# Differential attention of a two-block network on one Trainium2 core: the scores of heads 1 to 3 as three rounded products, and the outputs' sums of squares as halvings on GpSimd

## The reference

```python
q = rms_norm(q, g_q) * (HEAD_DK ** -0.5)
k = rms_norm(k, g_k)
...
        s = jnp.einsum('bqhjd,bkhjd->bhjqk', qi, k).astype(jnp.float32) + bias[None, :, None]
        p = jax.nn.softmax(s, axis=-1)
        w = (p[:, :, 0] - lam * p[:, :, 1]).astype(v.dtype)
        return jnp.einsum('bhqk,bkhd->bqhd', w, v)
...
    o = rms_norm(o, g_o) * (1.0 - lam_init)
```

## Time and profile before

| | us |
|---|---|
| median of 3 runs | 2111.61 (2109.74 to 2114.71) |
| the profiled execution, its own time | 2111.26 |
| the profiled execution, its span | 2109.5 |
| attention block, first score matmul to the next block's first matmul | 314.8 to 474.8 |
| busy in the whole span | PE 2035.7 (96%), DVE 1658.3 (79%), ACT 1081.6 (51%), POOL 262.5 (12%) |

### The profile page before, as it was taken

One profiled execution on the slowest core, in us unless ns is written; L12 is line 12 of the kernel. 1 busy time (PEld: TensorE's weight loads), 2 busy tenths in 40 slices (PEclk: granted clock), 3 DMA queues, 4 the chain that ended last, 5 costly groups with the idle time before them and its releaser, 6 DMA issues. The chain is left out here.

```text
span 2109.5 us, 25237 instructions
## 1 busy us (share of the span) xinstructions
PE 2035.7 (96%) x9940; PEld 1586.0 (75%) x9940; DVE 1658.3 (79%) x1706; ACT 1081.6 (51%) x1267; POOL 262.5 (12%) x192
## 2 busy tenths in 40 slices
PE   6999999999988999999999989999999999899998
PEld 4766766777736888888888757888888876688876
DVE  5575448885686999999999769999999977855776
ACT  4388417883236777777777542112222159622134
POOL 0200000001000111111110140000000006623040
PEclk9999999999999999999999999999999999999999
DMA  7311332104489999999999741111122236433121
GB/s 292 118 40 40 125 112 85 41 1 100 163 350 348 366 401 393 401 393 399 392 394 398 212 183 43 60 60 62 58 80 100 90 114 236 160 130 120 41 80 60
DMA packets 131496, 381.95 MB, mean 181 GB/s; under 512 B 9736, under 2 KB 22568, under 8 KB 131401
## 3 DMA queue, kind: packets, MB, share of 16 engines
q1 hardware_dynamic: 117640, 341.02, 42.7%
q0 software_dynamic: 7536, 22.70, 4.4%
q10 hardware_dynamic: 6224, 16.93, 2.0%
HBM read 337.49 MB, written 43.07 MB: 180 GB/s over the span
## 5 line engine op out<-in xcount | busy, mean ns | idle before, releaser
L2992 DVE SCALAR_TENSOR_TENSOR arena<-arena,vecs 128x1023 f32<-128x1023 f32 (+14 forms) x240 | 304.5, 1269 | 7.1
L2292 DVE TENSOR_TENSOR w_low<-W,w_high 128x2048 fp32r<-128x2048 f32 x96 | 217.0, 2288 | 33.5 <-ACT w_high L2189 33.5
L2292 DVE TENSOR_TENSOR w_low<-arena,w_high 128x2048 fp32r<-128x2048 f32 x96 | 218.4, 2290 | 19.0 <-ACT w_high L2189 19.0
L2005 PE MATMUL Q<-hT_high,w_high 128*128 128x512 f32 (+1 forms) x736 | 229.4, 391 | 2.6 <-DVE hT_low L2275 1.9
L2005 PE MATMUL Q<-hT_low,w_high 128*128 128x512 f32 (+1 forms) x720 | 224.5, 390 | 0.0
L2189 ACT ACTIVATE w_high<-arena 128x2048 fp32r<-128x2048 f32 x96 | 184.2, 1920 | 73.1 <-PE Q L2080 73.1
L2005 PE MATMUL Q<-hT_high,ring_low 128*128 128x512 f32 x704 | 219.7, 390 | 0.0
L2189 ACT ACTIVATE w_high<-W 128x2048 fp32r<-128x2048 f32 x96 | 184.0, 1919 | 66.4 <-PE Q L2080 64.3
L2018 ACT ACTIVATE w_high<-W 128x1024 fp32r<-128x1024 f32 x44 | 46.5, 1058 | 251.7 <-PE Q L2005 243.0
L2005 PEld LDWEIGHTS Q<-hT_high,w_high 128*128 128x128 f32 (+1 forms) x736 | 135.0, 184 | 35.1 <-DVE hT_low L2275 2.1
L2080 PE MATMUL Q<-w_high,x_high 128*128 128x512 f32 x512 | 160.9, 396 | 0.6 <-DVE x_low L2300 0.6
(11 more groups left out here) (502 smaller groups left out, 4148.7 us busy)
## 6 DMA issues: line engine op xcount, KB each, us to landing
arena<-in_w_dram SPq DMA_DIRECT2D x48, 2048.0 KB, 11.5
W<-in_w_dram SPq DMA_DIRECT2D x48, 2048.0 KB, 12.4
W<-in_w_mod_dram SPq DMA_DIRECT2D x12, 2048.0 KB, 8.2
W<-in_w_in_dram SPq DMA_DIRECT2D x12, 2048.0 KB, 8.4
W<-in_w_out_dram SPq DMA_DIRECT2D x6, 2048.0 KB, 9.8
spill<-arena ACTq DMA_DIRECT2D x24, 512.0 KB, 2.7
W<-in_w_in_dram SPq DMA_DIRECT2D x8, 1024.0 KB, 8.8
arena<-spill SPq DMA_DIRECT2D x3, 2048.0 KB, 12.4
```

Source lines behind the costliest of these rows:

```text
L2005: ins = nc.tensor.matmul(Q[rows, 2 * pair_of(n) + half, :], w[:, k], x[:, k, HALF * half:HALF * half + HALF], start=k == 0 and w is high a ...
L2292: nc.vector.tensor_tensor(wl[:], chunk_src(r, j), wh[:].bitcast(F32), ALU.subtract).then_inc(low_v, 1)
L2992: ins = nc.vector.scalar_tensor_tensor(conf[:, i, j:], u[:, 0:S - j], w, conf[:, i, j:], ALU.mult, ALU.add)
```

## The change

For heads 1 to 3, POOL splits q and k of a head into a rounded first part (`qk_first`, two pairs of tiles in turn) and the rest (`qk_low`, written over q and k themselves), by a copy and a subtraction each. The scores of these heads are then three products each, for two halves of the keys and two maps: 12 matmuls a turn in place of 4, j being the innermost loop. Heads 1 and 2 are split at the start of the block. Head 3 is split after POOL has done the square sums of turns 0 to 13 and PE the scores of turn 15, whose tiles it takes over. ACT no longer squares: `o_ready` is raised by the scaled copy, and POOL takes the sum of squares of each output by a product and seven additions of halves, each waiting for the one before.

```diff
-        o_square = tiles(23)[:, HALF:HALF + P]
+        SPLIT_HEADS = range(1, HEADS)
+        qk_low = rounded("qk_low", 24, [P, 2 * HEADS, S])
+        qk_first = [[rounded(f"qk_first{t}", t, [P, S]) for t in pair] for pair in ((6, 21), (22, 23))]
+        qk_split = sem("qk_split")
+        o_sq = keep[:, 2 * P:3 * P]
...
+                def square_sum(i):
+                    h, t = divmod(i, NT)
+                    pool.wait_ge(o_ready, i + 1)
+                    g_link(nc.gpsimd.tensor_tensor(o_sq, o_rows[:, h, t], o_rows[:, h, t], ALU.mult))
+                    for w in (P // 2, P // 4, P // 8, P // 16, P // 32, P // 64):
+                        g_link(nc.gpsimd.tensor_tensor(o_sq[:, 0:w], o_sq[:, 0:w], o_sq[:, w:2 * w], ALU.add))
+                    g_link(nc.gpsimd.tensor_tensor(o_ssq[:, i:i + 1], o_sq[:, 0:1], o_sq[:, 1:2], ALU.add))
+
+                for n, h in enumerate(SPLIT_HEADS):
+                    if n >= 2:
+                        for i in range(2 * NT - 2):
+                            square_sum(i)
+                        pool.wait_ge(score_mm, 2 * NT * (h - 1))
+                    for side in range(2):
+                        whole, first = qk[:, HEADS * side + h], qk_first[n % 2][side]
+                        nc.gpsimd.tensor_copy(first[:], whole).then_inc(qk_split, 1)
+                        pool.wait_ge(qk_split, 4 * n + 2 * side + 1)
+                        nc.gpsimd.tensor_tensor(qk_low[:, HEADS * side + h], whole, first[:].bitcast(F32), ALU.subtract)\
+                            .then_inc(qk_split, 1)
+                for i in range(2 * NT - 2, TURNS):
+                    square_sum(i)
...
+                def split_scores(i):
...
+                    pe.wait_ge(qk_split, 4 * n + 4)
+                    for half in range(2):
+                        cols_k = slice(HALF * half, HALF * half + HALF)
+                        for p, (q, k) in enumerate(((q_first, k_first), (q_first, k_low), (q_low, k_first))):
+                            for j in range(2):
+                                if half == 0 and p == 0:
+                                    pe.wait_ge(max_ready, 2 * (i - 1) + j + 1)
+                                rows = slice(DK * j, DK * j + DK)
+                                ins = nc.tensor.matmul(Q[:, 2 * j + half, :], q[rows, P * t:P * t + P], k[rows, cols_k],
+                                                       start=p == 0, stop=p == 2)
+                                if half == 1 and p == 2:
+                                    ins.then_inc(score_mm, 1)
...
-                    nc.scalar.activation(o_rows[:, h, t], Q[:, 6 + i % 2, 0:P], ACT.Copy, scale=over_sum)
-                    if i:
-                        act.wait_ge(o_ready, i)
-                    nc.scalar.activation(o_square, Q[:, 6 + i % 2, 0:P], ACT.Square, scale=over_sum,
-                                         accum_out=o_ssq[:, i:i + 1]).then_inc(o_ready, 1)
+                    nc.scalar.activation(o_rows[:, h, t], Q[:, 6 + i % 2, 0:P], ACT.Copy, scale=over_sum)\
+                        .then_inc(o_ready, 1)
```

More of the change, by code:

```diff
@@ L1222, in _ @@
+                for i in range(2 * NT - 2, TURNS):
+                    square_sum(i)
             @block.tensor
             def _(pe):
+                def split_scores(i):
+                    h, t = divmod(i, NT)
+                    n = SPLIT_HEADS.index(h)
+                    q_first, k_first = qk_first[n % 2]
+                    q_low, k_low = qk_low[:, h], qk_low[:, HEADS + h]
+                    pe.wait_ge(qk_split, 4 * n + 4)
[10 more added lines that the diff above has]
+                                    ins.then_inc(score_mm, 1)
@@ L1224, in scores @@
                 def scores(i):
                     h, t = divmod(i, NT)
+                    if h in SPLIT_HEADS:
+                        split_scores(i)
+                        return
                     for j in range(2):
```

## The result

The changed kernel took 2117.62 us in the median of ten runs (2116.24 to 2121.87, and one of 2449.76), the kernel before 2111.35 beside it: a ratio of 1.0033, 95% interval [1.0024, 1.0043]. It is slower, by some 7 us. The run of 2449.76 had a mean granted clock of 0.791, the others 0.985 to 0.989, and the ratio leaves it out. The profiled execution took 2117.37, its span is 2115.6, 6.1 longer than before.

The account below looks back on a forecast made before the run. PE was taken to bound the attention block, with DVE next at 0.4 us of slack. Terms -5.8 + 5.0 + 2.5 + 2.6 + 2.7 + 1.7 = +8.7 on 2111.26 gave 2120 us, range 2113 to 2128.

Parts of the forecast that it names:

- C: First turns: POOL's splits of heads 1 and 2 delay DVE's weights, +5.0 us (0 to 7).
- B: Eight turns with `out_rest`: L1193 waits for POOL's product, a turn taking 5.05 against 4.73, +2.6 us.
- the clock: Behind the block's end: PE at half clock after standing still, partly hidden by a later wait, +1.7 us.
- A: Scores of heads 1 to 3: fp32r pairs shorten a turn by 0.36 to 4.37 us; 16 turns give -5.8.
- D: Turns 16 or 17: POOL's split of head 3 delays DVE, +2.5 us (0 to 5).
- the sums: Block's end: POOL's last two square sums delay the next block's start, +2.7 us (1.3 to 3.8).
- The rival without them: Scores: fp32r pairs run one after the other, +1.0 us in 24 turns, +33 in all, 2145; chance 0.06.
- half as much POOL work: Head 3's split: half the POOL work of heads 1 and 2 was taken to cost half, +2.5 us.
- DVE needs 4.61: Turns with `out_rest`: DVE's chain, L1193 included, was read as needing 4.61 us against PE's 4.73.
- POOL's work in DVE's free stretches: Attention block: POOL's instructions miss DVE's two-input work, so C and D cost 0; -4.1 us, 2107.2; chance 0.20.
- Half contention: Block: one subtraction of heads 1 and 2 and one of head 3 hit at half length; +0.9, 2112.2; chance 0.12.

Follow-up runs that it names:

- e5: Kernel before plus four copies and four subtractions of k tiles on POOL at the block's start, into scratch; ratio 1.004 [1.0027, 1.0054].
- e4: Changed kernel with squares back on ACT and each split instruction gated behind chosen turns' weights; 2104.33 us against 2110.32 for the kernel before.
- e9: Kernel before plus the eight POOL instructions of e5, gated as in e4; ratio 1.0003 [0.9994, 1.0012].
- e1: Changed kernel with squares back on ACT, so POOL only splits, ungated; 2107.86 us against 2110.32 for the kernel before.
- e2: Kernel before with only the square sums moved to POOL, scores left float32 and unsplit; ratio 1.002 [1.0011, 1.003].
- e8: Changed kernel, square sums on POOL, with only its split instructions gated as in e4; 2107.84 us against 2111.46 for the kernel before.
- e10: Kernel before plus the eight POOL instructions of e5 done twice, ungated; ratio 1.0039 [1.0025, 1.0053] against the kernel before.
- e7: e4 with map j as the outermost loop of the split scores; ratio 1.0031 [1.0017, 1.0045] against the kernel before.

## Why the prediction was right, and where its sizes were off

The mechanism, POOL and DVE holding each other for one instruction at a time, was right, and so was the sign of each term; the sum came out at 2120.0 against 2117.62 (+8.7 forecast, +6.3 between the medians). That it came so near is in part luck: C, B and the clock were 5.1 us too high together, A, D and the sums 2.9 too low, and more than a third of D is a cost that the forecast did not have, PE's half clock behind a held turn inside the block. The terms:

**A, the scores: -5.4 for -5.8.** A turn of 4.39, saving 0.34. The passes of a pair are 0.233 us apart (392.56 to 393.49, four steps), not 0.227 as in the earlier trace rows. The Trainium skill's figure ("TensorE: Matmul & The Clock Gate", section "Back-to-back issue gap"), 216 ns, is the farther one; no run here shows it. The pairs ran side by side: the rival without them, 2145, is out.

**C, splits of heads 1 and 2: +3.8 for +5.0.** L1339 was held by 2.2 us in the first turn (3.46 for 1.28), by 0.7 in the second, with 0.46 and 0.73 at L1336; the third and fourth turns were free, since there the last subtraction waited for DVE. The forecast had DVE 3.2 and then 2.2 late; it was 2.6 and 1.5. e5 shows POOL as the cause, e4 and e9 show the place.

**D, split of head 3: +4.3 for +2.5.** The step that failed is "half as much POOL work" for "half of C". The cost goes by what POOL has in flight when a turn's weights come up, and by what PE's clock does then. Turn 16 lost 2.6: a copy held L1336 by 0.65 and a subtraction L1339 by 2.2, with 0.2 of slack. The turn behind it lost 1.65, and there it was PE at half clock and not DVE, a term that the forecast put at nothing inside the block. In e1 the same work falls two turns earlier, L1324 is held by 0.86 and L1327 by 0.73, the clock stays up, and 1.4 is lost; in e4 nothing is.

**B, turns with `out_rest`: +0.3 for +2.6.** The largest miss. "DVE needs 4.61" was read from a turn in which L1193 waited a little; alone DVE needs 4.54 (e4), and without POOL the eight turns would have gained 1.8 (e1, e4). And POOL's product does not cost its length: after L1339 it ends 0.26 later (432.99 and 1.44 against 432.89 and 1.28), and L1197 is 0.2 longer, not 0.44. So the turns take 4.67 and 4.96 by turns, for 5.05.

**E, the sums: +3.4 for +2.7.** A square sum takes 2.55 us from its product to its end (476.29 to 478.84), 2.4 forecast, and two stand behind the next to last output. PE follows after 0.67 and not 0.46. e2 has the same 3.4 by itself.

**E, the clock: +0.1 for +1.7.** The clock did fall to 0.50, the level of 1.2 GHz, after PE's gap, but at 476.90, inside the gap, and PE's work fills only 4.22 of the 6.83 us at that level. PE falls back by 2.0 there, from 4.72 us behind the kernel before to 6.71 (486.15 for 479.44), and where the wait of the earlier trace rows is gone it gets 1.9 back: 4.84 (507.55 for 502.70). From the block's end to the next long wait it is 118.39 us for 117.85, and the other 0.4 of that arises near its end, PE before and after:

```profile
588.13 0.64 PE L1492 MATMUL Q<-arena,keep 128*32 128x128 f32 x16 [0.56 <-ACT arena L1609]
```

```profile
592.95 1.08 PE L1535 MATMUL Q<-arena,keep 128*32 128x128 f32 x16 [0.56 <-ACT arena L1652]
```

In the changed kernel the granted clock falls to 0.50 at 592.95, ahead of this work; in the kernel before it falls at 590.77, behind it. Why it fell earlier is not shown.

**The rivals.** POOL's work in DVE's free stretches was a possible course (2107.2), and is what e8 arranges (2107.84); unaided it does not come about, not in the change, e1, e5 or e10. Half contention, 2112.2, is out: one subtraction held L1339 at its full length in turn 0 and one in turn 16 (3.46 and 3.48 for 1.28).

What stays open: why e1's low clock lasts longer than that of the changed kernel behind a like gap.

## What to carry to other kernels

Work on GpSimd that reads SBUF is not free because its queue is empty: price each of its instructions by what VectorE has in flight at that moment, and hang it behind a VectorE instruction that is followed by work on PSUM, as the gates here (-3.6 us against the kernel before in medians with the sums, -6.0 with ScalarE's squares). If it can't be placed, cut it: VectorE waits for an instruction, not for the columns. Read a chain's need from a stretch where that engine is the bound, and put a serial reduction behind a block's last output only where someone else still works.

## What the runs showed of the hardware

- A GpSimd copy or subtraction holds also a VectorE instruction on one column (0.22 us becomes 0.68 to 0.95), and is held itself (a copy of 1.04 takes 2.04 beside L1339, at 324.34). Memsets of 0.95 and 1.80 us hold nothing, and the maxima, which read PSUM, keep their 1.21 beside either.
- A held VectorE is felt a second time: behind 2.31 and 2.57 us in which TensorE waited for it, the granted clock was 0.50 for some us (1.65 us in the turn behind turn 16; in e1's first turns 1.4 us more than in the changed kernel). Behind 1.32 us (e1, head 3) it stayed at 1.00.
- Two fp32r matmuls on 64 rows each run side by side, a pair every 0.233 us, also where the program has them four places apart, but not six (e4, e7).
